# Second layer's gate and up projections as 20 units of seven block products, with the sums made by VectorE

## The chip, the cores and the metric

One Trainium2 chip, one of its cores. The metric is the device time of one launch in microseconds, lower is better. Engines are called as in the profile: PE (TensorE), DVE (VectorE), ACT (ScalarE), POOL (GpSimd), SP (SyncE, which only issues loads here).

## The reference, cut to what matters

Four transformer-like layers in fp32 over 512 tokens of width 1024. The change lies in the feed-forward part of the second one (`layer_c`):

```python
def swiglu(h, wg, wu, wd):
    return (jax.nn.silu(h @ wg) * (h @ wu)) @ wd
...
    h = modulate(x, norm_ffn, sh_f, sc_f)
    return x + g_f[:, None, :] * swiglu(h, wg, wu, wd)
```

`wg` and `wu` are 1024x2816, `wd` is 2816x1024. `modulate` is an RMS norm with a gain, a scale and a shift for each channel.

## The kernel before, in words

**Layout.** Activations lie transposed, channels on partitions: `x` is 8 blocks (k) of 128 channels by 512 tokens. Each weight comes as a panel of 128 output channels and 8 k-blocks, 128x1024 on chip (512 KB). A ring of four slots holds `raw`, `w_hi` and `w_lo`.

**Precision.** Each product is made of three matmuls in the fast fp32r format (L679 to L681): w_hi with h_hi, w_hi with h_lo, w_lo with h_hi. hi is the rounded value, lo the rest. ACT makes `w_hi` from `raw` (`split_hi`, L1226), POOL makes `w_lo = raw - w_hi` (`split_lo`, L603), and the activations' parts come from ACT (`h_hi`, `g_hi`) and DVE (`h_lo`, `g_lo`).

**What sets the order.** Every engine runs an order written out by hand, in step through counting semaphores. SP loads panel p+4 once `lo_ready` has reached p+1. ACT splits it once PE is done with the slot's old panel (`panel_done`). PE waits for `lo_ready` and for `bank_free` of the PSUM bank p % 4.

**The feed-forward part.** 22 tiles of 128 hidden channels go in parts of 8, 8 and 6. A part has first a gate and an up panel for each tile (`panels`, 48 matmuls of 512 columns for a pair), then 8 down panels over the part's tiles. For a tile ACT takes SiLU of the gate's bank (L1283), DVE multiplies it with the up bank (L1776), ACT rounds the product to `g_hi` (L1291), DVE takes the rest to `g_lo` (L1791). `add_x` (L1702) adds a down panel to `x`. At the start of the part DVE's `norm_h` makes the normalized `tn`, ACT `h_hi` (L1252), DVE `h_lo` (L1686), k by k, and PE goes through three panels at once (`by_k`), then the fourth. POOL only splits here. The loads of three constants of the third layer (`wsT`, `rows`, `bs`) are issued by ACT before the second layer's output projection; POOL's `affine_select` (L658) waits for them after the last down panel.

## Time and profile before

| | us |
|---|---|
| median of 3 runs (lowest, highest) | 2456.07 (2455.55, 2458.01) |
| profiled execution, span | 2452.9 |
| PE busy | 2386.9 (97%) |
| DVE, ACT, POOL busy | 1291.4, 951.4, 1097.8 |
| mean granted TensorE clock | 0.986 |

The profiled execution's time is its span, from the first to the last instruction; the runs' times are of whole launches. PE's busy time counts pipelined matmuls that overlap; how fast they follow each other is read from their starts.

### The profile page before, as it was taken

To read this page: it belongs to the slowest core of one execution; us is meant where nothing else is said; L and a number is where in the kernel's file an instruction comes from. 1 tells how busy PE (TensorE), PEld (TensorE's weight loads), DVE (VectorE), ACT (ScalarE), POOL (GpSimd) and SP (SyncE) were. 2 spreads that over 40 slices of the span, in tenths; PEclk is the share of its full clock that TensorE was granted. 3 is DMA by queue.
4 is the path that set the end of the run, shared out by engine and by line. 5 is a ranking of instruction groups with operands and counts; after the bars stand their busy time and mean duration, and the time that the engine had idled before them with its cause. 6 is when DMAs were issued, how large, how long until landed. Compare 5 with 4: busy or idle time off the path is not lost.

```text
span 2452.9 us, 34883 instructions
## 1 busy us (share of the span) xinstructions
PE 2386.9 (97%) x11957; PEld 1933.5 (79%) x11957; DVE 1291.4 (53%) x2318; ACT 951.4 (39%) x1554; POOL 1097.8 (45%) x529
## 2 busy tenths in 40 slices
PE   7999999999999999999999999999999999999998
PEld 6776778888876577888888678888888968888887
DVE  6777564443248753111147966454567474635455
ACT  3458332222335834222235454222246384422222
POOL 2336334444535543444455733444354464444433
PEclk9999999999999999999999999999999999999999
DMA  7531335554222022222222212322232201232222
GB/s 301 203 129 53 129 138 191 186 179 146 103 78 86 19 86 77 95 94 95 102 99 91 78 68 104 108 91 101 94 112 95 95 19 61 86 111 94 96 93 77
DMA packets 64196, 261.54 MB, mean 107 GB/s; under 512 B 7248, under 2 KB 7760, under 8 KB 57936
## 3 DMA queue, kind: packets, MB, share of 16 engines
q1 hardware_dynamic: 61056, 251.00, 28.8%
q10 hardware_dynamic: 3024, 8.98, 1.0%
q8 instruction: 74, 1.21, 0.2%
q14 instruction: 42, 0.34, 0.0%
HBM read 257.86 MB, written 2.10 MB: 106 GB/s over the span
## 4 chain that ended last, share of the span: by engine, by line
PE 88%; DVE 5%; issue 3%; POOL 1%; ACT 1%; DMA 1%; POOLq 1%; DVEq 0%; SPq 0%; ACTq 0%
PE bank L679 26%; PE bank L680 26%; PE bank L681 26%; PE bank L872 2%; PE bank L862 2%; PE bank L891 2%; POOL w_lo L603 1%; DMA first_mods<-in_first 1%; DVE acc L1639 1%; POOLq L667 1%; DVE bank L2268 1%; DVE bank L1908 1%; PE bank L804 1%; PE bank L700 1%; POOL prob L620 0%
## 5 line engine op out<-in xcount | busy, mean ns | idle before, releaser
L603 POOL TENSOR_TENSOR w_lo<-raw,w_hi 128x1024 fp32r<-128x1024 f32 x378 | 917.5, 2435 | 1219.0 <-ACT w_hi L1226 1217.3
L679 PE MATMUL bank<-h_hi,w_hi 128*128 128x512 f32 x1760 | 698.2, 397 | 13.8 <-DVE h_lo L1686 7.8
L680 PE MATMUL bank<-h_lo,w_hi 128*128 128x512 f32 x1760 | 690.4, 392 | 0.0
L681 PE MATMUL bank<-h_hi,w_lo 128*128 128x512 f32 x1760 | 690.3, 392 | 0.0
L1226 ACT ACTIVATE w_hi<-raw 128x1024 fp32r<-128x1024 f32 x378 | 392.5, 1051 | 424.3 <-PE bank L681 421.5
L679 PE MATMUL bank<-g_hi,w_hi 128*128 128x512 f32 x1072 | 418.5, 390 | 0.0
L681 PE MATMUL bank<-g_hi,w_lo 128*128 128x512 f32 x1072 | 417.2, 389 | 0.0
L680 PE MATMUL bank<-g_lo,w_hi 128*128 128x512 f32 x1072 | 417.1, 389 | 0.0
L679 PEld LDWEIGHTS bank<-h_hi,w_hi 128*128 128x128 f32 x1760 | 333.9, 190 | 94.9 <-DVE h_lo L1686 8.7
L681 PEld LDWEIGHTS bank<-h_hi,w_lo 128*128 128x128 f32 x1760 | 333.6, 190 | 71.5
L680 PEld LDWEIGHTS bank<-h_lo,w_hi 128*128 128x128 f32 x1760 | 333.7, 190 | 68.0 <-issue 0.5
L681 PEld LDWEIGHTS bank<-g_hi,w_lo 128*128 128x128 f32 x1072 | 201.2, 188 | 42.4
L679 PEld LDWEIGHTS bank<-g_hi,w_hi 128*128 128x128 f32 x1072 | 201.2, 188 | 41.5 <-issue 0.2
L680 PEld LDWEIGHTS bank<-g_lo,w_hi 128*128 128x128 f32 x1072 | 201.3, 188 | 41.3
L1776 DVE TENSOR_TENSOR prod<-silu,bank 128x512 f32<-128x512 f32 x44 | 30.2, 687 | 304.0 <-PE bank L681 303.8
L620 POOL TENSOR_TENSOR prob<-prob,stat 128x1024 f32<-128x1024 f32 (+1 forms) x96 | 120.0, 1253 | 90.7 <-DVE stat L1826 56.8
L1291 ACT ACTIVATE g_hi<-prod 128x512 f32 x66 | 41.7, 632 | 300.9 <-DVE prod L1776 197.3
L1702 DVE SCALAR_TENSOR_TENSOR x<-bank,plain,x 128x512 f32<-128x512 f32 x64 | 47.6, 748 | 156.8 <-PE bank L681 156.8
L1908 DVE SCALAR_TENSOR_TENSOR bank<-modraw,csil,bank 128x256 f32<-128x256 f32 x222 | 108.6, 489 | 16.9 <-issue 0.4
L1312 ACT ACTIVATE prob<-prob,stat 128x512 f32<-128x512 f32 (+1 forms) x192 | 106.7, 558 | 27.1 <-DVE stat L1816 26.6
L1702 DVE SCALAR_TENSOR_TENSOR x<-bank,modv,x 128x512 f32<-128x512 f32 x64 | 47.3, 748 | 120.7 <-PE bank L681 119.9
L1816 DVE CUSTOM_DVE_ANT_0 prob<-bank,mask 128x512 f32<-128x512 f32 (+1 forms) x192 | 90.2, 486 | 37.2 <-PE bank L862 33.7
(299 smaller groups left out, 2542.6 us busy)
## 6 DMA issues: line engine op xcount, KB each, us to landing
raw<-in_panels SPq DMA_DIRECT2D x378, 512.0 KB, 3.5
modraw<-in_pairs SPq DMA_DIRECT2D x40, 1024.0 KB, 5.6
first_mods<-in_first SPq DMA_DIRECT2D x4, 2048.0 KB, 22.2
x<-in_x SPq DMA_DIRECT2D x1, 2048.0 KB, 9.5
w<-in_w ACTq DMA_DIRECT2D x1, 2048.0 KB, 8.4
out<-yout ACTq DMA_DIRECT2D x8, 256.0 KB, 2.2
mask<-in_causal ACTq DMA_DIRECT2D x1, 1024.0 KB, 4.8
mask<-in_dilated ACTq DMA_DIRECT2D x1, 1024.0 KB, 7.5
```

Of the source, the lines that this page charges most:

```text
L603: pool.tensor_tensor(w_lo[:, slot, :], raw[:, slot, :], w_hi[:, slot, :].bitcast(F32), ALU.subtract)\
L620: pool.tensor_tensor(both, both, stat[:, 2, u:u + 2].rearrange("p (b o) -> p b o", o=1) .broadcast_to((P, 2, w)), ALU.mult).then_inc(weigh ...
L679: pe.matmul(out, w_h, m_h, start=start, stop=False)
L680: pe.matmul(out, w_h, m_l, start=False, stop=False)
L681: return pe.matmul(out, w_l, m_h, start=False, stop=stop)
L862: pe.matmul(score_bank(run, n, b)[:, 0:w], q_of(run, pairs_[n], b), k_of(run, pairs_[n], b), start=True, stop=True).then_inc(score_ready, 1)
L872: m = pe.transpose(bank[2 + b][:, P * j:P * j + P], prob[:, PROB_SLOT[n % PROB_STEPS], b, P * j:P * j + P], ident[:, :])
L1226: act.activation(w_hi[:, slot, :], raw[:, slot, :], ACT.Copy).then_inc(hi_ready, 1)
L1312: act.activation(row, row, ACT.Exp, bias=stat[:, 0, u % 64:u % 64 + 1], scale=-1.0, accum_out=stat[:, 1, u % 64:u % 64 + 1]).then_inc(exp_ ...
L1702: dve.scalar_tensor_tensor(out=x[:, n, :], in0=bank[p % RING][:, :], scalar=scale_by, in1=x[:, n, :], op0=MUL, op1=ADD).then_inc(bank_free, 1)
L1816: dve.tensor_tensor_reduce(row_of(n, b, w), score_bank(run, n, b)[:, 0:w], mask[:, i, 0:w], -SCALE, HIGHEST, ADD, ALU.min, stat[:, 0, u % ...
L1908: m = dve.scalar_tensor_tensor(out=part if k < KB - 1 else to, in0=w[:, :, k, :], scalar=csil[:, k:k + 1], in1=part, op0=MUL, op1=ADD)
```

## The change

The gate and up panels of a tile, stacked, are a matrix of 1024x256. It is cut in four: B11 and B21 are the gate panel's k-blocks 0 to 3 and 4 to 7, B12 and B22 the same of the up panel. The activations are cut by k in the same way, and the 512 tokens into early and late halves. Where four blocks times four blocks need eight block products, Strassen's algorithm (here with shared sums) needs seven, P1 to P7, each of 4 k-blocks, 3 matmuls a block and 256 columns. The first four panels (two tiles) stay as they were; the other 20 tiles are units (6, 8 and 6 in the three parts).

- DVE makes four differences of weight blocks for each unit, into `wdiff`, one unit ahead (`weight_sums`).
- ACT and POOL split seven 128x512 halves for a unit, P1, P2 and P3's from `raw`, the other four from `wdiff` (`half_high`, `half_low`).
- Once, after the norm, DVE makes four sums of the normalized activations (now kept whole in `tn8`) and their lo parts, ACT their hi parts (`activation_sums`, `sums_high`).
- PE goes P7, P2, P6, P1 of the next unit, P5, P4, P3. P1 goes to bank X and is copied by ACT to bank Y (seed); P2 completes X, the early gate. P6 is added to Y. ACT copies P7 to `seventh`; DVE adds it to Y into bank Z (waited for by `third_ready`); P4 completes Z, the late gate. P5 is added to Y; DVE adds `seventh` again, which gives `late_up`; P3 completes Y, the early up part.
- The three constant loads are issued by ACT behind the last unit.

```diff
+UNITS = (PARTS[0] - PLAIN_FIRST // 2,) + PARTS[1:]
+ORDER = ("P1", "P7", "P2", "P6", "P5", "P4", "P3")
...
+        WDIFF = {"P5": 0, "P7": 1, "P6": 2, "P4": 3}
...
+        def weight_half(part, name, u):
+            p = unit_panel(part, u)
+            if name in WDIFF:
+                return wdiff[u % 2][:, WDIFF[name], :]
+            of, at = {"P1": (0, 0), "P2": (0, 1), "P3": (1, 1)}[name]
+            return raw[:, (p + of) % RING, KH * P * at:KH * P * at + KH * P]
...
-            split_from(P_OUT1 + RING, P_AG - P_OUT1 - RING)
+            split_from(P_OUT1 + RING, P_FFN1 + PLAIN_FIRST - P_OUT1 - RING)
+            def half_low(part, name, u):
+                source = weight_half(part, name, u)
+                hi, lo = half_of(w_hi, name), half_of(w_lo, name)
+                if name == "P3":
+                    pool.wait_ge(hi_ready, unit_panel(part, u) + 2)
+                    pool.tensor_tensor(lo, source, hi.bitcast(F32), ALU.subtract).then_inc(lo_ready, 2)
+                else:
+                    pool.wait_ge(half_hi, made(part, name, u) + 1)
+                    pool.tensor_tensor(lo, source, hi.bitcast(F32), ALU.subtract).then_inc(half_lo, 1)
+            for part, n in enumerate(UNITS):
+                down = unit_panel(part, n)
+                for name in ORDER:
+                    half_low(part, name, 0)
+                for u in range(n):
+                    last = u == n - 1
+                    if u == 0:
+                        half_low(part, "P1", 1)
+                    if not last:
+                        half_low(part, "P7", u + 1)
+                        half_low(part, "P2", u + 1)
+                        half_low(part, "P6", u + 1)
+                        if u + 2 < n:
+                            half_low(part, "P1", u + 2)
+                        half_low(part, "P5", u + 1)
+                        half_low(part, "P4", u + 1)
+                        half_low(part, "P3", u + 1)
+                split_from(down, KB)
...
+            def product(part, name, u, out, fresh=False):
+                if name == "P3":
+                    pe.wait_ge(lo_ready, unit_panel(part, u) + 2)
+                else:
+                    pe.wait_ge(half_lo, made(part, name, u) + 1)
+                (m_hi, m_lo), wh, wl = moving_of(name), half_of(w_hi, name), half_of(w_lo, name)
+                for k in range(KH):
+                    ks = slice(P * k, P * k + P)
+                    pe.matmul(out, wh[:, ks], m_hi[:, k, :], start=(fresh and k == 0), stop=False, skip_group_check=True)
+                    pe.matmul(out, wh[:, ks], m_lo[:, k, :], start=False, stop=False, skip_group_check=True)
+                    m = pe.matmul(out, wl[:, ks], m_hi[:, k, :], start=False, stop=(k == KH - 1), skip_group_check=True)
+                if name == "P3":
+                    m.then_inc(panel_done, 2)
+                else:
+                    m.then_inc(half_used, 1)
...
+            def units(part):
...
+                if part == 0:
+                    for out in (Y_BANK[0], Z_BANK):
+                        pe.matmul(bank[out][:, :], h_hi[:, 0, 0:P], h_hi[:, 0, :], start=True, stop=True)
+                first_product(part, 0)
+                for u in range(n):
+                    x_out, y_out = unit_out(X_BANK[u % 2]), unit_out(Y_BANK[u % 2])
+                    pe.wait_ge(sum_lo, 1)
+                    if before + u:
+                        pe.wait_ge(seventh_copied, before + u)
+                    product(part, "P7", u, unit_out(SEVENTH_BANK), True)
+                    pe.wait_ge(seeded, before + u + 1)
+                    product(part, "P2", u, x_out)
+                    pe.wait_ge(sum_lo, 3)
+                    product(part, "P6", u, y_out)
+                    if u + 1 < n:
+                        first_product(part, u + 1)
+                    pe.wait_ge(third_ready, before + u + 1)
+                    product(part, "P5", u, y_out)
+                    product(part, "P4", u, unit_out(Z_BANK))
+                    pe.wait_ge(sum_lo, 4)
+                    pe.wait_ge(late_up_ready, before + u + 1)
+                    product(part, "P3", u, y_out)
...
+            def half_high(part, name, u):
...
+                if name in WDIFF:
+                    order = ("P7", "P5", "P6", "P4").index(name)
+                    act.wait_ge(wdiff_ready, 4 * (units_before(part) + u) + order + 1)
+                else:
+                    p = unit_panel(part, u) + (name == "P3")
+                    act.wait_ge(raw_landed[p % RING], 16 * (p // RING + 1))
+                m = act.activation(half_of(w_hi, name), weight_half(part, name, u), ACT.Copy)
+                if name == "P3":
+                    m.then_inc(hi_ready, 2)
+                else:
+                    m.then_inc(half_hi, 1)
...
+                seed(0)
+                for u in range(n):
+                    f, last = unit_tile(part, u), u == n - 1
+                    if u == 0:
+                        half_high(part, "P1", 1)
+                    act.wait_ge(half_used, used(part, "P7", u) + 1)
+                    if before + u:
+                        act.wait_ge(late_up_ready, before + u)
+                    act.activation(seventh[:, :], unit_out(SEVENTH_BANK), ACT.Copy).then_inc(seventh_copied, 1)
+                    if not last:
+                        half_high(part, "P7", u + 1)
...
+                    if f % PARTS[0]:
+                        tile_high(f - 1)
+                    act.wait_ge(half_used, used(part, "P2", u) + 1)
+                    act.activation(silu[:, f % 2, 0:HALF], unit_out(X_BANK[u % 2]), ACT.Silu).then_inc(early_silu, 1)
+                    if not last:
+                        half_high(part, "P2", u + 1)
+                        half_high(part, "P6", u + 1)
+                        seed(u + 1)
+                        if u + 2 < n:
+                            half_high(part, "P1", u + 2)
+                        half_high(part, "P5", u + 1)
...
+                    act.wait_ge(half_used, used(part, "P4", u) + 1)
+                    act.activation(silu[:, f % 2, HALF:T], unit_out(Z_BANK), ACT.Silu).then_inc(silu_ready, 1)
+                    if not last:
+                        half_high(part, "P4", u + 1)
+                        half_high(part, "P3", u + 1)
...
-            act.dma_start(wsT[:, :, :], A["wsT"]).then_inc(layer2_landed, 16)
-            act.dma_start(rows[:, :, :], A["rows"]).then_inc(layer2_landed, 16)
-            act.dma_start(bs[:, :, :], A["bs"]).then_inc(layer2_landed, 16)
             project(P_OUT1, 3)
             take_root(3)
             h_high(3)
-            ffn(1, P_FFN1, 3)
+            sums_high()
+            ffn_by_units(P_FFN1)
...
+            def weight_sums(part, u):
+                p, before = unit_panel(part, u), units_before(part) + u
+                for q in (p, p + 1):
+                    dve.wait_ge(raw_landed[q % RING], 16 * (q // RING + 1))
+                if u >= 2:
+                    dve.wait_ge(half_lo, made(part, "P4", u - 2) + 1)
+                to = wdiff[u % 2]
+                b11, b21 = (raw[:, p % RING, KH * P * w:KH * P * w + KH * P] for w in range(2))
+                b12, b22 = (raw[:, (p + 1) % RING, KH * P * w:KH * P * w + KH * P] for w in range(2))
+                dve.tensor_tensor(to[:, WDIFF["P7"], :], b22, b12, SUB).then_inc(wdiff_ready, 1)
+                dve.tensor_tensor(to[:, WDIFF["P5"], :], b12, b11, SUB).then_inc(wdiff_ready, 1)
+                dve.drain()
+                dve.tensor_tensor(to[:, WDIFF["P6"], :], b22, to[:, WDIFF["P5"], :], SUB).then_inc(wdiff_ready, 1)
+                dve.drain()
+                dve.tensor_tensor(to[:, WDIFF["P4"], :], b21, to[:, WDIFF["P6"], :], SUB).then_inc(wdiff_ready, 1)
+            def sum_low(n, of):
+                dve.wait_ge(sum_hi, n)
+                hi = sum4[:, 0, :, :] if of == 4 else sums_hi[:, of - 1, :, :]
+                to = sum4[:, 1, :, :] if of == 4 else sums_lo[:, of - 1, :, :]
+                dve.tensor_tensor(to, sum_a[of][:, :, :], hi.bitcast(F32), SUB).then_inc(sum_lo, 1)
+            def activation_sums():
+                late = slice(HALF, T)
+                at = MOD + 3 * KB
+                dve.tensor_tensor(shift12[:, :], modv[:, at:at + KH], modv[:, at + KH:at + KB], ADD)
+                dve.tensor_tensor(sum_a[3][:, :, :], tn8[:, 0:KH, 0:HALF], tn8[:, 0:KH, late], SUB).then_inc(sum_made, 1)
+                dve.drain()
+                for k in range(KH):
+                    m = dve.scalar_tensor_tensor(out=sum_a[1][:, k, :], in0=tn8[:, k, late], scalar=shift12[:, k:k + 1],
+                                                 in1=tn8[:, KH + k, late], op0=ADD, op1=ADD)
+                m.then_inc(sum_made, 1)
+                sum_low(1, 3)
+                dve.drain()
+                for k in range(KH):
+                    m = dve.scalar_tensor_tensor(out=sum_a[2][:, k, :], in0=sum_a[1][:, k, :], scalar=shift(3, k),
+                                                 in1=tn8[:, k, 0:HALF], op0=SUB, op1=SUB)
...
+                sum_low(3, 2)
+                dve.drain()
+                sum_low(4, 4)
...
+            def units(part):
+                n, before = UNITS[part], units_before(part)
+                def finish(u):
+                    f = unit_tile(part, u)
+                    dve.wait_ge(panel_done, unit_panel(part, u) + 2)
+                    dve.wait_ge(early_silu, before + u + 1)
+                    dve.tensor_tensor(prod[:, f % 2, 0:HALF], silu[:, f % 2, 0:HALF], unit_out(Y_BANK[u % 2]), MUL)\
+                        .then_inc(bank_free, 2)
+                    dve.wait_ge(silu_ready, FC + f + 1)
+                    dve.tensor_tensor(prod[:, f % 2, HALF:T], silu[:, f % 2, HALF:T], late_up[:, :], MUL).then_inc(prod_ready, 1)
+                for u in range(n):
+                    f = unit_tile(part, u)
+                    if u:
+                        finish(u - 1)
+                    if u + 1 < n:
+                        weight_sums(part, u + 1)
+                    if u or part == 0:
+                        tile_low(f - 1)
+                    dve.wait_ge(half_used, used(part, "P6", u) + 1)
+                    dve.wait_ge(seventh_copied, before + u + 1)
+                    if before + u:
+                        dve.wait_ge(silu_ready, FC + f)
+                    dve.tensor_tensor(unit_out(Z_BANK), unit_out(Y_BANK[u % 2]), seventh[:, :], ADD).then_inc(third_ready, 1)
+                    dve.wait_ge(half_used, used(part, "P5", u) + 1)
+                    dve.tensor_tensor(late_up[:, :], unit_out(Y_BANK[u % 2]), seventh[:, :], ADD).then_inc(late_up_ready, 1)
+                    dve.drain()
+                finish(n - 1)
+                dve.drain()
+                tile_low(unit_tile(part, n - 1))
+                dve.drain()
```

**On DVE**, one steady unit. Before, the loop's second tile and its end (`prod` is SiLU times the up bank):

```order
L1774 REGISTER_ALU
L1775 REGISTER_ALU [waits silu_ready]
L1776 TENSOR_TENSOR prod<-silu,bank 128x512 [waits panel_done]
L1791 ISA [waits f_hi_ready]
L1791 TENSOR_TENSOR g_lo<-prod,g_hi 128x512
L1770 REGISTER_ALU
L1770 COMPARE_AND_BRANCH
```

Now:

```order
L2185 TENSOR_TENSOR prod<-silu,bank 128x256 [waits early_silu,panel_done]
L2188 TENSOR_TENSOR prod<-silu,late_up 128x256 [waits silu_ready]
L2121 TENSOR_TENSOR wdiff_152<-raw 128x512 [waits half_lo,raw_landed1,raw_landed0]
L2122 TENSOR_TENSOR wdiff_152<-raw 128x512
L2124 TENSOR_TENSOR wdiff_152<-raw,wdiff_152 128x512
L2126 TENSOR_TENSOR wdiff_152<-raw,wdiff_152 128x512
L2166 TENSOR_TENSOR g_lo<-prod,g_hi 128x512 [waits f_hi_ready]
L2202 TENSOR_TENSOR bank<-bank,seventh 128x256 [waits silu_ready,seventh_copied,half_used]
L2204 TENSOR_TENSOR late_up<-bank,seventh 128x256 [waits half_used]
```

Between one tile's product and its g_lo now stand the four differences for the next unit, and the addition into Z comes behind g_lo.

**On ACT**, from the second layer's norm into the first units. Before:

```order
L1252 ACTIVATE h_hi<-tn,modv 128x512 [waits t_ready] x8
L1278 UNCONDITIONAL_BRANCH
L1278 ISA
L1283 ACT_TABLE_LOAD
L1283 ACTIVATE silu<-bank 128x512 [waits panel_done]
L1222 ISA
L1226 ACTIVATE w_hi<-raw 128x1024 [waits panel_done,raw_landed2]
```

Now:

```order
L1437 ACTIVATE h_hi<-tn_144,modv 128x512 [waits t_ready] x8
L1487 ACTIVATE sums_hi<-sum_147 128x1024 [waits sum_made]
L1487 ACTIVATE sums_hi<-sum_145 128x1024 [waits sum_made]
L1487 ACTIVATE sums_hi<-sum_146 128x1024 [waits sum_made]
L1487 ACTIVATE sum_150<-sum_147 128x1024 [waits sum_made]
L1498 ACT_TABLE_LOAD
L1498 ACTIVATE silu<-bank 128x512 [waits panel_done]
L1476 ACTIVATE w_hi<-raw 128x512 [waits raw_landed2,panel_done]
L1476 ACTIVATE w_hi<-wdiff_151 128x512 [waits wdiff_ready,panel_done]
L1476 ACTIVATE w_hi<-raw 128x512 [waits raw_landed2,panel_done]
```

The four hi parts of the sums and the table load for SiLU now stand ahead of the first SiLU and of the first halves' hi parts.

**On POOL**, the second layer's splits. Before, the loop over panels and what follows it:

```order
L603 TENSOR_TENSOR w_lo<-raw,w_hi 128x1024 [waits hi_ready]
L602 REGISTER_ALU
L603 TENSOR_TENSOR w_lo<-raw,w_hi 128x1024 [waits hi_ready]
L602 REGISTER_ALU
L603 TENSOR_TENSOR w_lo<-raw,w_hi 128x1024 [waits hi_ready]
L602 REGISTER_ALU
L603 TENSOR_TENSOR w_lo<-raw,w_hi 128x1024 [waits hi_ready]
L608 REGISTER_ALU
L608 COMPARE_AND_BRANCH
L658 ISA
L658 AFFINE_SELECT wsT<-wsT 128x1024 [waits layer2_landed]
```

Now, from the last plain panels to P1 and P7 of unit 1:

```order
L693 TENSOR_TENSOR w_lo<-raw,w_hi 128x1024 [waits hi_ready]
L698 REGISTER_ALU
L698 COMPARE_AND_BRANCH
L756 TENSOR_TENSOR w_lo<-raw,w_hi 128x512 [waits half_hi]
L756 TENSOR_TENSOR w_lo<-wdiff_151,w_hi 128x512 [waits half_hi]
L756 TENSOR_TENSOR w_lo<-raw,w_hi 128x512 [waits half_hi]
L756 TENSOR_TENSOR w_lo<-wdiff_151,w_hi 128x512 [waits half_hi] x3
L753 TENSOR_TENSOR w_lo<-raw,w_hi 128x512 [waits hi_ready]
L756 TENSOR_TENSOR w_lo<-raw,w_hi 128x512 [waits half_hi]
L756 TENSOR_TENSOR w_lo<-wdiff_152,w_hi 128x512 [waits half_hi]
```

Where one subtraction for a panel stood, a unit has seven of half the size, and all seven of unit 0 stand ahead of the first of unit 1 (the row after L753).

## Rows read from the trace of the kernel before

**Rows 1.** The page, part 1: busy us (share of the span) xinstructions

```profile
PE 2386.9 (97%) x11957; PEld 1933.5 (79%) x11957; DVE 1291.4 (53%) x2318; ACT 951.4 (39%) x1554; POOL 1097.8 (45%) x529
```

**Rows 2.** The page, part 4: the chain that ended last, by line

```profile
PE bank L679 26%; PE bank L680 26%; PE bank L681 26%; PE bank L872 2%; PE bank L862 2%; PE bank L891 2%; POOL w_lo L603 1%; DMA first_mods<-in_first 1%; DVE acc L1639 1%; POOLq L667 1%; DVE bank L2268 1%; DVE bank L1908 1%; PE bank L804 1%; PE bank L700 1%; POOL prob L620 0%
```

**Rows 3.** Busy time by engine in a stretch of the second layer's feed-forward part

```profile
core 0: us, PE busy (x) PEld busy (x) DVE busy (x) ACT busy (x) POOL busy (x), PEclk, DMA share, GB/s
1000.00:1290.00 290.00, 290.00 (x1281) 240.15 (x1280) 56.36 (x72) 83.70 (x104) 129.38 (x56) 1.00 0.28 98
```

**Rows 4.** Timeline of PE, 512 columns: start, us; 36 matmuls apart

```profile
1179.67 0.39 PE L680 MATMUL bank<-g_lo,w_hi 128*128 128x512 f32 x1
...
1187.83 0.39 PE L680 MATMUL bank<-g_lo,w_hi 128*128 128x512 f32 x1
```

**Rows 5.** Timeline of PE, 256 columns (an earlier stage); 26 matmuls apart

```profile
723.83 0.28 PE L679 MATMUL bank<-w_hi,h_hi 128*128 128x256 f32 x1
...
726.95 0.28 PE L681 MATMUL bank<-w_hi,h_lo 128*128 128x256 f32 x1
```

**Rows 6.** Groups of instructions by shape, whole run: busy us, mean ns, idle before

```profile
L603 POOL TENSOR_TENSOR w_lo<-raw,w_hi 128x1024 fp32r<-128x1024 f32 x378 | 917.5, 2435 | 1219.0 <-ACT w_hi L1226 1217.3 <-issue 1.4
L634 POOL TENSOR_TENSOR h_lo<-ya,h_hi 128x512 fp32r<-128x512 f32 x4 | 5.1, 1274 | 0.0
L1776 DVE TENSOR_TENSOR prod<-silu,bank 128x512 f32<-128x512 f32 x44 | 30.2, 687 | 304.0 <-PE bank L681 303.8 <-issue 0.3
L1851 DVE TENSOR_TENSOR h_lo<-bank,h_hi 128x256 fp32r<-128x256 f32 x24 | 9.9, 411 | 2.2 <-ACT h_hi L1338 2.2
L1908 DVE SCALAR_TENSOR_TENSOR bank<-modraw,csil,bank 128x256 f32<-128x256 f32 x222 | 108.6, 489 | 16.9 <-issue 0.4
L1226 ACT ACTIVATE w_hi<-raw 128x1024 fp32r<-128x1024 f32 x378 | 392.5, 1051 | 424.3 <-PE bank L681 421.5 <-DMA raw<-in_panels 2.4
L1291 ACT ACTIVATE g_hi<-prod 128x512 f32 x66 | 41.7, 632 | 300.9 <-DVE prod L1776 197.3 <-DVE prod L1788 103.6
L1338 ACT ACTIVATE h_hi<-bank 128x256 fp32r<-128x256 f32 x24 | 8.9, 371 | 2.6 <-PE bank L891 2.6
```

**Rows 7.** Timelines of DVE and POOL where they meet: start, us

```profile
1272.46 2.87 DVE L1639 TENSOR_TENSOR acc<-acc,sq 128x512 f32<-128x512 f32 x1
1272.40 2.39 POOL L603 TENSOR_TENSOR w_lo<-raw,w_hi 128x1024 fp32r<-128x1024 f32 x1 [1.37 <-ACT w_hi L1226]
1282.09 1.40 DVE L1639 TENSOR_TENSOR acc<-acc,sq 128x512 f32<-128x512 f32 x1
1282.92 2.83 POOL L603 TENSOR_TENSOR w_lo<-raw,w_hi 128x1024 fp32r<-128x1024 f32 x1
951.84 0.69 DVE L1776 TENSOR_TENSOR prod<-silu,bank 128x512 f32<-128x512 f32 x1 [2.22 <-PE bank L681]
946.66 10.38 POOL L603 TENSOR_TENSOR w_lo<-raw,w_hi 128x1024 fp32r<-128x1024 f32 x4 [23.45 <-ACT w_hi L1226]
```

**Rows 8.** Timelines of DVE and ACT at the start of the part

```profile
936.53 1.59 DVE L1686 SCALAR_TENSOR_TENSOR h_lo<-tn,modv,h_hi 128x512 fp32r<-128x512 f32 x2
937.22 1.28 ACT L1283 ACT_TABLE_LOAD   x1
945.04 0.60 ACT L1283 ACTIVATE silu<-bank 128x512 f32<-128x512 f32 x1 [6.54 <-PE bank L681]
```

**Rows 9.** Gaps of PE, each with the stretch behind it (columns of rows 3)

```profile
337.23 0.61 PE L700 MATMUL bank<-ones,modsum 128*128 128x1 f32 x4 [1.97 <-DVE modsum L1908]
338.73:342.15 3.42, 3.42 (x10) 2.65 (x9) 0.69 (x1) 2.37 (x3) 2.25 (x1) 0.50 0.91 353
1411.72 1.12 PE L1140 MATMUL bank<-cout,ones 128*128 128x512 f32 x2 [2.25 <-DVE cout L2268]
1413.90:1417.30 3.40, 2.19 (x8) 1.37 (x9) 3.19 (x5) 0.63 (x1) 0.00 (x0) 1.00 0.00 0
```

More of the change, by code:

```diff
@@ L837, in ffn @@
                         begun = 4
-                    panels(p + begun, 2 * size - begun, *up, mods=p < MOD_UNTIL)
+                    if layer == 1:
+                        units(n)
+                    else:
+                        panels(p + begun, 2 * size - begun, *up, mods=p < MOD_UNTIL)
                     p += 2 * size
@@ L1301, in ffn @@
                     else:
[L1302 removed]
+                        project_folded(p, 8)
                     p += KB
```

183 lines of the change are left out of this document (176 added, 7 removed).

## The prediction

> **What bounds the kernel now.** I read the page's first part first: TensorE (PE) is busy 97% of the span [rows 1]. Then the chain that ended last: nearly four fifths of it are the three matmul lines of the hi/lo product [rows 2]. Then the stretch that the change touches, the second layer's feed-forward part, about 927 to 1300 us: from 1000 to 1290 PE is busy all of the time at the full granted clock, while VectorE (DVE) works 56 us of 290, ScalarE (ACT) 84 and GpSimd (POOL) 129 [rows 3]. No other engine is waited for there, so one microsecond of matmul taken out is one microsecond gained, as long as the others stay out of the way. The argument below is that they don't.
>
> **What PE saves.** A gate and up pair costs 2 x 8 x 3 = 48 matmuls of 512 columns. They start (1187.83 - 1179.67)/36 = 0.2267 us apart [rows 4], so a pair is 10.88 us. A unit has seven products of 4 x 3 = 12 matmuls with 256 columns, 84 in all. Such matmuls stand elsewhere in the trace: (726.95 - 723.83)/26 = 0.1200 us apart [rows 5], with a weight load before each, as here. A unit is then 10.08 us. A product is 1.44 us. Twenty units save 20 x 0.80 = 16.0 us; two extra 512-column matmuls ahead of the first unit cost 0.45.
> Halving the columns does not halve the spacing. The Trainium skill (TensorE: Matmul & The Clock Gate, "Back-to-back issue gap") gives N/2.4 + 2.5 ns, so 216 and 109 ns, which would save 20 x (10.36 - 9.17) = 24 us. The rows have some 11 ns more for each matmul, and a unit has 36 matmuls more than a pair; the rows decide, and by the page the sum below would be 8 us lower.
>
> **What the other engines get.** Per unit POOL gets seven subtractions of 128x512 in place of two of 128x1024. One such took 1.27 us against 2.44 [rows 6], so 8.9 us in place of 4.9. DVE gets four subtractions of weights from SBUF (0.69 each, by the 128x512 products of rows 6), two PSUM additions and two products of 256 columns (0.41 each), and keeps the 0.69 of g_lo: some 5.1 us. ACT gets seven 128x512 copies (0.63 each), four short PSUM passes (about 0.4) and g_hi: 6.6 us. Each engine alone fits into 10.08 us. Together DVE and POOL don't.
>
> **The wait between DVE and POOL.** A DVE addition with both inputs in SBUF, issued at 1272.46 just after a POOL subtraction had started, ended at 1275.33, 0.54 us after POOL's end at 1274.79; alone it takes 0.69. In the other direction, POOL's subtraction of 1282.92 ended at 1285.75, 2.26 us after the DVE addition before it (1283.49), in place of 2.40 from its own start [rows 7]. So the later one waits for the earlier one's end and then needs 0.54 (DVE) or its own time less 0.14 (POOL; 1.27 becomes 1.13). A DVE product with one input in PSUM took 0.69 beside POOL's row of four [rows 7]: those are not held.
> The Trainium skill says the same (SBUF — State Buffer, "Who interferes with whom": a DVE instruction with two SBUF inputs contends with a GpSimd instruction that reads SBUF, and the second fully blocks). By this rule, as by the rows, the change puts six such DVE instructions and seven such POOL ones into one unit: it speaks against the change.
>
> Now one steady unit, in time from the end of the previous unit's P3, which is when P7 starts. PE needs P7, P2, P6 and the next unit's P1, 5.76 us, before it asks for third_ready. DVE must do, in this order: early product 0.2 to 0.6 (0.2 is the tail of the last matmul); late product, held by POOL's P4 half until 1.1, ends 1.4; first weight subtraction, held by POOL's P3 half until 2.5, ends 3.1; second 3.8; third 4.5. POOL's P7 half (its hi part is ready near 3.9, since ACT needs the first subtraction for it) then takes its turn until 5.65; fourth subtraction 6.2; POOL's P2 half until 7.35; g_lo 7.9; the addition into Z 8.3. P5 can start at 8.45. PE has stood since 5.76: **2.7 us**. P5, P4, P3 follow, 4.32, so a unit is 12.8 us. Without POOL the same DVE row ends near 4.9 and PE never waits.
> The wait stands in every unit but the first of a part: there no product of a previous unit goes ahead (in the first part that unit is part of the start, below). In the last unit of a part there are no weight subtractions, but no next P1 either, so PE asks at 4.32 and g_lo comes after ACT's 1.05 us panel split: 2.3. That is 14 x 2.7 + 3 x 2.3 = **44.7 us**.
>
> **The start.** After the last h_lo (938.12) [rows 8] DVE makes the first unit's weight differences (4 x 0.69 with drains, 2.9), then the activation sums: up to the last of them three instructions over 1024 elements (no row of its own; 0.41 at 256 and 0.69 at 512 columns give 1.25) and three groups of four 128x256 steps (0.49 each, 1.9 a group), 12.4 in all, so 950.5. ACT then has the last sum's hi part (1.05), a table load (1.28; before, it ran at 937.22 where nobody waited), SiLU (0.60) and P1's hi half (0.63), and POOL 1.27: 955.5. PE ends the four plain panels 24 x 0.2267 after by_k's end at 945.04 [rows 8], at 950.5, and the two extra matmuls at 950.9. It waits **4.6 us**. Next, POOL has all seven halves of unit 0 ahead of P1 of unit 1: 7 more at 1.23 and some five DVE turns of 0.54 make 966.8, and PE, having done P1, P7, P2 and P6 as their halves come, wants it near 962 to 963: **4 us**.
>
> **The clock.** Granted clock falls to half (0.50, the 1.2 GHz level) after an idle PE: after the 1.97 us gap that ends at 337.23 it was 0.50 from 338.73 for 3.42 us; after the 2.25 us gap that ended at 1411.72 it stayed at 1.00 [rows 9]. The gaps here are 2.3 to 4.6 us long, so I take it for half of the 19 gaps, at half of 3.42 = 1.7 each: **+16**. Bounds: none 0, all 32.
>
> **Nothing, and what covers it.** The panels' loads are as many; SP now releases them in twos when P3's low half is done, 10 us before the first reader, against a landing of a few microseconds (DMA share 0.28 [rows 3]). The three layer-2 constant loads move behind the last unit, eight down panels ahead of POOL's wait for them; if that cover went, they would cost POOL about one landing. The down panels are unchanged; their first-panel waits for the last tile are covered by size-1 tiles, except in the last part, about 1 us.
>
> **Sum.** -16.0 + 0.5 + 44.7 + 4.6 + 4 + 16 + 1 = +54.8, of which I take 53, since a slow clock after a gap also gives POOL time. Span 2452.9 + 53 = 2506. The median of the runs, 2456.07, stands 3.1 above the profiled span, so **2509 us**.
>
> **Rivals.**
> A, only the shared turn counts. If DVE's turns fell where POOL waits for ACT anyway, the unit would be bound by the sum of turns, 5 x 0.54 + 0.27 + 7 x 1.13 = 10.9 us, as long as a pair before: with the start (9) and little clock, 2456 + 12 = 2468; between that and the forecast every mixture is possible. For it: turns may interleave better than I laid them out. Against: DVE's order is fixed, with third_ready last.
> B, every gap lowers the clock, and the halved PE makes the next unit's DVE work late too: +16 more, 2525.
> C, the other side: DVE is held at most once in a unit, since POOL's halves come when DVE waits for PE. Then third_ready comes before 5.76 + a little: -16 + 0.5 + 8.6 = 2449, faster. It decides where the held time per unit is under 0.9 us (5.76 - 4.9); rows 7 have single holds of 1.1 and more for a POOL half, and POOL is busy 8.9 of 10 us, so DVE's six instructions can hardly miss it.
> D, the POOL halves are the bound by themselves (if a 128x512 one costs more than 1.44 us when held back): then 7 x 1.68 (1.13 + 0.54) = 11.8 a unit, 2456 + 18 + 9 + some clock, 2490.
>
> **Numbers.** Forecast (2490 to 2522) 0.60; A and mixtures up to 2490 0.15; D 0.08, inside the lower end; B 0.08; C 0.06; nearly no change 0.03. The range, 2478 to 2528, takes in the forecast with clock losses from 0 to 32, D and most of B. A difference of 0.2%, 5 us, is what a measurement of this kernel can tell: faster 0.06, same 0.04, slower 0.90.
>
> **What would show it.** Right: in the stretch of the units PE idle before P5's first matmul, released by DVE's addition into bank 7, 2 to 3 us, in 17 units; DVE's weight subtractions with means over 1.1 us in place of 0.69; unit period near 12.8; one gap of 4 to 5 us near 951 released by POOL; new stretches of clock 0.50. Wrong: DVE two-input instructions at 0.7 us beside POOL, unit period under 11, or PE waiting for POOL's halves (rival D) rather than for DVE.

## The result, and the profile after

The changed kernel takes 2509.06 us (median of 4 runs, 2507.12 to 2510.97), the kernel before 2455.99 in the same comparison (2455.55 to 2458.01): ratio 1.0212, 95% interval 1.0199 to 1.0224. That is 53.1 us slower. The profiled executions, spans 2505.4 and 2452.9, stand 52.5 apart.

The page of the changed kernel, part 1 (it answers to [rows 1]):

```profile
PE 2394.4 (96%) x12679; PEld 1973.8 (79%) x12679; DVE 1439.5 (57%) x2476; ACT 1007.9 (40%) x1715; POOL 1210.0 (48%) x629
```

PE's busy time hardly grew; it now stands idle or runs slowly for some 50 us more. DVE is busy 148 us more and POOL 112; part of that is time in which they are held, as shown below. The same stretch as in [rows 3], busy time by engine, then one slow stretch within it:

```profile
1000.00:1290.00 290.00, 258.44 (x1688) 240.59 (x1687) 144.96 (x158) 109.67 (x203) 200.58 (x126) 0.95 0.27 88
```

```profile
1112.39:1115.81 3.42, 3.21 (x15) 3.21 (x16) 0.40 (x2) 0.24 (x1) 2.17 (x2) 0.50 0.00 0
```

PE was busy 290 of 290 us at clock 1.00 before; now 258 of 290 at a mean of 0.95. DVE went from 56 to 145 us and POOL from 129 to 201: neither is full. So what holds PE is an order of waiting, and the view of PE's waits in the feed-forward part, 925 to 1355 us, names it (waited for; us in total, times, longest):

```profile
PE bank L960 <- DVE bank L2202: 38.0, 17, 2.6
PE bank L960 <- POOL w_lo L756: 7.4, 2, 4.8
...
PE bank L799 <- DVE g_lo L2166: 0.8, 1, 0.8
```

L2202 is DVE's addition into bank Z, `third_ready`. PE waits for it exactly 17 times, in no first unit of a part. (The line left out was there before the change too.) PE's timeline at the first matmul of P5 in three units that follow one another:

```profile
1100.00 0.39 PE L960 MATMUL bank<-sums_hi,w_hi 128*128 128x256 f32 x1 [2.57 <-DVE bank L2202]
...
1112.60 0.58 PE L960 MATMUL bank<-sums_hi,w_hi 128*128 128x256 f32 x1 [2.27 <-DVE bank L2202]
...
1126.58 0.38 PE L960 MATMUL bank<-sums_hi,w_hi 128*128 128x256 f32 x1 [2.26 <-DVE bank L2202]
```

A unit is 12.60 us here at full clock, and 13.98 where, as behind 1112.60, the clock is at 0.50 (its 1.2 GHz level) right after the gap. Until 932 us the clock is at 0.50 before the change too. Behind that there are twelve slow stretches in the part, one of 6.8 us at 962 and eleven of 3.4; before there was none. Each of the eleven begins between 0.4 us before and 1.6 us after the end of one of the 17 gaps; the other six gaps, 1.9 to 2.6 us long like these, are followed by none, and nothing read here tells the two sorts apart.

The start of P7 in the unit between the first two of those gaps, then DVE in that unit and POOL beside it (the timelines of the three engines; they answer to [rows 7]):

```profile
1104.42 0.28 PE L960 MATMUL bank<-sums_hi,w_hi 128*128 128x256 f32 x1
```

```profile
1104.67 0.42 DVE L2185 TENSOR_TENSOR prod<-silu,bank 128x256 f32<-128x256 f32 x1 [2.51 <-PE bank L962]
1105.01 0.72 DVE L2188 TENSOR_TENSOR prod<-silu,late_up 128x256 f32<-128x256 f32 x1
1105.65 1.78 DVE L2121 TENSOR_TENSOR wdiff<-raw 128x512 f32<-128x512 f32 x1
1107.36 0.68 DVE L2122 TENSOR_TENSOR wdiff<-raw 128x512 f32<-128x512 f32 x1
1108.13 0.69 DVE L2124 TENSOR_TENSOR wdiff<-raw,wdiff 128x512 f32<-128x512 f32 x1
1108.92 1.61 DVE L2126 TENSOR_TENSOR wdiff<-raw,wdiff 128x512 f32<-128x512 f32 x1
1110.45 1.75 DVE L2166 TENSOR_TENSOR g_lo<-prod,g_hi 128x512 fp32r<-128x512 f32 x1
1112.13 0.42 DVE L2202 TENSOR_TENSOR bank<-bank,seventh 128x256 f32<-128x256 f32 x1
```

```profile
1104.16 1.29 POOL L756 TENSOR_TENSOR w_lo<-wdiff,w_hi 128x512 fp32r<-128x512 f32 x1 [0.42 <-ACT w_hi L1476]
1105.44 1.44 POOL L753 TENSOR_TENSOR w_lo<-raw,w_hi 128x512 fp32r<-128x512 f32 x1
1108.24 1.74 POOL L756 TENSOR_TENSOR w_lo<-wdiff,w_hi 128x512 fp32r<-128x512 f32 x1 [1.35 <-ACT w_hi L1476]
1109.95 1.71 POOL L756 TENSOR_TENSOR w_lo<-raw,w_hi 128x512 fp32r<-128x512 f32 x1
```

From the early product on DVE has no gap over 0.1 us. Three of its instructions with 512 columns are held: L2121 ends at 1107.43, 0.55 after POOL's end at 1106.88; L2126 at 1110.53, 0.55 after POOL's 1109.98; L2166 at 1112.20, 0.54 after POOL's 1111.66. So is the late product, L2188, of 256 columns: it took 0.72 in place of 0.42 and ended 0.28 after POOL's 1105.45. L2122 and L2124 fell where POOL waited for ACT, or began just ahead of its next one, and took their own 0.69; POOL's, held in turn, took 1.71 to 1.74 in place of 1.27. The groups by shape, whole part (busy us, mean ns, idle before), show the same over 20 units:

```profile
L2166 DVE TENSOR_TENSOR g_lo<-prod,g_hi 128x512 fp32r<-128x512 f32 x22 | 42.1, 1912 | 11.1 <-ACT g_hi L1493 11.1
L2121 DVE TENSOR_TENSOR wdiff<-raw 128x512 f32<-128x512 f32 x20 | 29.9, 1496 | 0.4 <-issue 0.4
L2126 DVE TENSOR_TENSOR wdiff<-raw,wdiff 128x512 f32<-128x512 f32 x20 | 29.4, 1472 | 1.8
L2122 DVE TENSOR_TENSOR wdiff<-raw 128x512 f32<-128x512 f32 x20 | 19.1, 957 | 0.0
L2124 DVE TENSOR_TENSOR wdiff<-raw,wdiff 128x512 f32<-128x512 f32 x20 | 18.0, 902 | 2.2 <-issue 0.4
L2188 DVE TENSOR_TENSOR prod<-silu,late_up 128x256 f32<-128x256 f32 x20 | 14.2, 709 | 0.0
```

The five instructions of 512 columns with both operands in SBUF should take 0.69 each [rows 6]; the addition from PSUM takes its 0.42 (L2202 in the timeline). The start, which answers to [rows 8]: the last sum's hi part on ACT, with the table load, SiLU and P1's hi half behind it, then PE's two waits for POOL:

```profile
948.80 1.06 ACT L1487 ACTIVATE sum<-sum 128x1024 fp32r<-128x1024 f32 x1 [1.84 <-DVE sum L2155]
```

```profile
953.70 0.38 PE L960 MATMUL bank<-h_hi,w_hi 128*128 128x256 f32 x1 [2.56 <-POOL w_lo L756]
...
964.71 0.55 PE L960 MATMUL bank<-h_hi,w_hi 128*128 128x256 f32 x1 [4.84 <-POOL w_lo L756]
```

### The profile page after: what moved, and what is told of

Its sections match the earlier page's. It is cut to its first block, busy times and chain, and to the rows that moved or that the text cites. A ratio compares the mean times of both kernels' runs of the same rounds, so it can differ in the third digit from the quotient of the medians.

```text
span 2505.4 us, 36734 instructions
## 1 busy us (share of the span) xinstructions
PE 2394.4 (96%) x12679; PEld 1973.8 (79%) x12679; DVE 1439.5 (57%) x2476; ACT 1007.9 (40%) x1715; POOL 1210.0 (48%) x629
## 4 chain that ended last, share of the span: by engine, by line
PE 81%; DVE 9%; issue 4%; POOL 2%; ACT 1%; DVEq 1%; DMA 1%; POOLq 1%; SPq 0%; ACTq 0%
PE bank L799 22%; PE bank L801 22%; PE bank L800 22%; PE bank L1057 2%; PE bank L1047 2%; PE bank L1076 2%; PE bank L960 2%; PE bank L961 2%; PE bank L962 2%; DVE g_lo L2166 1%; DVE wdiff L2121 1%; POOL w_lo L693 1%; DMA first_mods<-in_first 1%; DVE acc L1938 1%; POOLq L787 1%
## 5 line engine op out<-in xcount | busy, mean ns | idle before, releaser
L693 POOL TENSOR_TENSOR w_lo<-raw,w_hi 128x1024 fp32r<-128x1024 f32 x338 | 823.2, 2444 | 1060.2 <-ACT w_hi L1411 1058.9
L799 PE MATMUL bank<-h_hi,w_hi 128*128 128x512 f32 x1440 | 573.8, 398 | 13.8 <-DVE h_lo L1988 7.8
L800 PE MATMUL bank<-h_lo,w_hi 128*128 128x512 f32 x1440 | 565.9, 393 | 0.0
L801 PE MATMUL bank<-h_hi,w_lo 128*128 128x512 f32 x1440 | 565.5, 393 | 0.0
L1411 ACT ACTIVATE w_hi<-raw 128x1024 fp32r<-128x1024 f32 x338 | 350.5, 1051 | 393.5 <-PE bank L801 384.7
L799 PEld LDWEIGHTS bank<-h_hi,w_hi 128*128 128x128 f32 x1440 | 273.5, 190 | 82.2 <-issue 8.7
L801 PEld LDWEIGHTS bank<-h_hi,w_lo 128*128 128x128 f32 x1440 | 273.5, 190 | 58.9
L800 PEld LDWEIGHTS bank<-h_lo,w_hi 128*128 128x128 f32 x1440 | 273.6, 190 | 55.8 <-issue 0.5
L799 PEld LDWEIGHTS bank<-g_hi,w_hi 128*128 128x128 f32 x1072 | 201.3, 188 | 42.8 <-DVE g_lo L2166 1.2
L756 POOL TENSOR_TENSOR w_lo<-wdiff,w_hi 128x512 fp32r<-128x512 f32 x80 | 118.5, 1484 | 54.8 <-ACT w_hi L1476 54.8
L960 PE MATMUL bank<-sums_hi,w_hi 128*128 128x256 f32 x240 | 74.5, 310 | 38.0 <-DVE bank L2202 38.0
```

The costliest lines, as they stand in the source:

```text
L693: pool.tensor_tensor(w_lo[:, slot, :], raw[:, slot, :], w_hi[:, slot, :].bitcast(F32), ALU.subtract)\
L756: pool.tensor_tensor(lo, source, hi.bitcast(F32), ALU.subtract).then_inc(half_lo, 1)
L799: pe.matmul(out, w_h, m_h, start=start, stop=False)
L800: pe.matmul(out, w_h, m_l, start=False, stop=False)
L801: return pe.matmul(out, w_l, m_h, start=False, stop=stop)
L960: pe.matmul(out, wh[:, ks], m_hi[:, k, :], start=(fresh and k == 0), stop=False, skip_group_check=True)
```

## The experiments

The theory: DVE's instructions with both operands in SBUF and POOL's halves take turns; with `third_ready` behind six of them PE waits in every unit, and each wait can lower its clock besides. Eight kernels test that, in two comparisons with the kernel before (2456.88 us in the first, 2456.42 in the second).

**1. No weight differences.**

```diff
-            if name in WDIFF:
-                return wdiff[u % 2][:, WDIFF[name], :]
-            of, at = {"P1": (0, 0), "P2": (0, 1), "P3": (1, 1)}[name]
+            of, at = {"P1": (0, 0), "P2": (0, 1), "P3": (1, 1), "P4": (0, 1), "P5": (1, 0), "P6": (1, 1), "P7": (1, 0)}[name]
...
-                        weight_sums(part, u + 1)
...
```

> Leaves out the four weight differences of each unit on VectorE; the halves P4 to P7 are split from the raw blocks instead, so the output is not the reference's. All seven GpSimd halves, the activation sums and the order stay. Theory (VectorE and GpSimd take turns, and third_ready comes last): the differences are four of VectorE's six held instructions; without them third_ready comes near 4 us into the unit and PE no longer waits in the steady units (38.0 us of PE's waits in the units fall to under 3, of the 12 stretches of clock 0.50 between 960 and 1310 at most two remain). What stays is the wait of some 5 to 7 us at the start and the saving of 16: 2450 to 2457 us. Rival 1 (GpSimd's seven halves are a bound by themselves): PE waits for w_lo in the units, 2480 or more. Rival 2 (VectorE's chain behind PE, the additions and ACT's passes, is too long even with no differences): over 1.5 us of wait in each unit remains, 2480 or more.

Measured: 2456.39 us, ratio 1.0003 (0.9993 to 1.0012). PE's waits in the units, the second of them in the first unit:

```profile
PE bank L958 <- DVE bank L2194: 5.1, 8, 1.1
PE bank L958 <- POOL w_lo L754: 3.5, 1, 3.5
```

Both rivals fall: POOL still makes seven halves a unit and behind the first unit nobody waits for it, and the chain through ACT and the additions is short enough. The waits for DVE are 5.1 us where under 3 was expected: g_lo (1.40 us on average) is still held. Two slow stretches are left of the twelve, as expected.

**2. GpSimd's halves a quarter as long.**

```diff
-                    pool.tensor_tensor(lo, source, hi.bitcast(F32), ALU.subtract).then_inc(half_lo, 1)
+                    pool.tensor_tensor(lo[:, 0:P], source[:, 0:P], hi[:, 0:P].bitcast(F32), ALU.subtract).then_inc(half_lo, 1)
...
```

> GpSimd's seven subtractions of a unit work on 128 of their 512 columns; the rest of w_lo keeps old values, so the output is not the reference's. VectorE's instructions are all there. Theory (the turn with GpSimd): a difference is held for a quarter of the time, VectorE's four differences go back from 0.9 to 1.5 us each to 0.7 to 0.9, third_ready comes before PE asks for it; waits of PE in the units under 4 us in all, 2448 to 2456 us. Rival (VectorE has simply too much work ahead of the addition, whatever GpSimd does): the addition comes no more than 0.5 us earlier in a unit, PE's waits stay over 25 us, 2490 or more.

Measured: 2452.96 us, ratio 0.9984 (0.9975 to 0.9994). PE's waits for the addition, and one of DVE's groups:

```profile
PE bank L960 <- DVE bank L2202: 5.7, 3, 1.9
```

```profile
L2121 DVE TENSOR_TENSOR wdiff<-raw 128x512 f32<-128x512 f32 x20 | 13.8, 688 | 0.4 <-issue 0.4
```

DVE does all its work here, and PE waits for its addition only in the last unit of each of the three parts: 5.7 us, and 2.4 for others at the start, where under 4 was expected. DVE has not too much to do; it is held. One difference (L2122, 0.94 us on average) stayed a little above the 0.9 expected.

**3. The addition earlier.**

```diff
                 dve.drain()
+                if between is not None:
+                    between()
                 dve.tensor_tensor(to[:, WDIFF["P6"], :], b22, to[:, WDIFF["P5"], :], SUB).then_inc(wdiff_ready, 1)
...
+                    def third():
...
+                        dve.tensor_tensor(unit_out(Z_BANK), unit_out(Y_BANK[u % 2]), seventh[:, :], ADD).then_inc(third_ready, 1)
                     if u + 1 < n:
-                        weight_sums(part, u + 1)
-                    if u or part == 0:
-                        tile_low(f - 1)
...
+                        weight_sums(part, u + 1, third)
...
                     dve.tensor_tensor(late_up[:, :], unit_out(Y_BANK[u % 2]), seventh[:, :], ADD).then_inc(late_up_ready, 1)
+                    if u or part == 0:
+                        tile_low(f - 1)
```

> Nothing left out. On VectorE the addition into bank Z (third_ready) moves from behind the four differences and g_lo to between the second and the third difference; the addition for late_up comes behind the fourth, g_lo last. The same work and the same turns. Theory (it is the place of the addition behind the held instructions that costs): the wait of 2.2 us in 17 units goes or falls under 0.7 us, and with it most of the slow stretches (12 now): 2455 to 2466 us. Rival 1 (the sum of turns bounds the unit, 10.9 us or more): the wait moves to another instruction, PE waits for w_lo or late_up by 0.8 us or more a unit, 2470 to 2490. Rival 2 (the cost is mostly in the clock and the start, not in the wait): under 15 us gained, 2494 or more.

Measured: 2460.82 us, ratio 1.0016 (1.0007 to 1.0026), +3.9 us in place of +53.1, with the same instructions. PE's waits, busy time in a stretch of units, and DVE around the addition:

```profile
PE bank L960 <- POOL w_lo L756: 7.4, 2, 4.9
PE bank L960 <- DVE bank L2201: 5.6, 10, 0.6
```

```profile
1100.00:1150.00 50.00, 47.62 (x383) 46.11 (x383) 44.60 (x42) 25.32 (x54) 50.00 (x33) 1.00 0.31 106
```

```profile
1119.52 1.78 DVE L2122 TENSOR_TENSOR wdiff<-raw 128x512 f32<-128x512 f32 x1
1121.49 0.43 DVE L2201 TENSOR_TENSOR bank<-bank,seventh 128x256 f32<-128x256 f32 x1 [0.19 <-PE bank L962]
1121.84 1.15 DVE L2126 TENSOR_TENSOR wdiff<-raw,wdiff 128x512 f32<-128x512 f32 x1
```

The view names PE as what the addition waited for, but P6, which it reads, had ended near 1119.93; DVE was in the held second difference until 1121.30. PE waits 0.6 us for the addition. Of the 17 distances between units within the parts, eight are 11.1 to 11.2 us; in the stretch shown, where they are, POOL is busy 50.00 of 50 us. That is close to the 10.9 that the prediction's rival A worked out as the sum of turns. So the turns by themselves cost some 1.1 us in such a unit, and their place ahead of `third_ready` the other 1.4. Over all 17 distances, from the first late_up addition of a part to its last, it is 177.2 us against 167.0 of PE's own work: the turns cost 10 us, and their place some 33 of the 42.8 worked out further down.

**4. The start in another order.**

```diff
                     act.activation(to, sum_a[of][:, :, :], ACT.Copy).then_inc(sum_hi, 1)
+                    if n == 1:
+                        half_high(0, "P1", 0)
+                        half_high(0, "P7", 0)
+                    if n == 2:
+                        half_high(0, "P2", 0)
+                        half_high(0, "P6", 0)
...
-                half_high(0, "P1", 0)
-                half_high(0, "P7", 0)
-                half_high(0, "P2", 0)
-                half_high(0, "P6", 0)
```

> Nothing left out. Only the start: ACT makes the hi parts of the halves P1 and P7 of the first unit after the second sum's hi part, P2 and P6 after the third's, ahead of the table load and SiLU, in place of behind them. Theory: the first wait of PE for w_lo (about 4.8 us of 7.4) falls by 2 to 4 us, but the activation sums by VectorE come no earlier and PE waits for them instead, so the time falls by 0 to 4 us: 2505 to 2509. Rival (the start's order is what the change lost by, through the clock too): 8 us or more gained, 2501 or less.

Measured: 2510.90 us (2509.64 to 2512.24), no gain, and 1.9 above the range expected. The wait has moved, not gone; PE now waits for ACT's copy of bank X into Y, which stands behind the last sum's hi part, the table load and the plain tiles' SiLU:

```profile
PE bank L960 <- ACT bank L1521: 6.3, 1, 6.3
```

The sums themselves come later too. The four steps of the last sum on DVE, in the changed kernel and here:

```profile
947.10 1.67 DVE L2155 SCALAR_TENSOR_TENSOR sum<-tn,modv,sum 128x256 f32<-128x256 f32 x4
...
949.77 3.75 DVE L2157 SCALAR_TENSOR_TENSOR sum<-tn,modv,sum 128x256 f32<-128x256 f32 x4
```

Here POOL makes two halves beside them (950.24 to 953.24), and the sum before it took 3.74 in place of 1.67 beside two others: the turn again, some 4 us of it, in a place where the changed kernel had none.

**5. The gap filled.** Before `pe.wait_ge(third_ready, ...)`:

```diff
+                    if u:
+                        for _ in range(18):
+                            pe.matmul(bank[S0][:, 0:HALF], h_hi[:, 0, 0:P], h_hi[:, 0, 0:HALF], start=True, stop=True)
                     pe.wait_ge(third_ready, before + u + 1)
```

> The result stays the same; added are 18 matmuls of 256 columns (18 x 0.12 = 2.16 us) on data at hand, into an idle PSUM bank, ahead of PE's wait for third_ready in the 17 units that wait. Nothing else of the changed kernel is touched, so VectorE's addition still comes when it did. Theory (the granted clock falls because PE stands, and this costs some 12 to 18 us beside the waits themselves): PE's waits for VectorE shrink to a few us, the stretches of 0.50 inside the units go, a unit stays at 12.6 to 12.9 us, and the time falls to 2492 to 2500 us. Rival (the clock falls in this part for another reason, or its cost lies inside the waits and is no extra): the time stays at 2507 to 2512.

Measured: 2495.09 us (2494.36 to 2495.79), ratio to before 1.0162 (1.0145 to 1.0179), so +38.7 in place of +53.1: 306 matmuls that nobody needs make the kernel 14.4 us faster. PE's waits for the addition fall to 0.9 us. Busy time in the same stretch as above, and the late_up additions of four units (their first and last start):

```profile
1000.00:1290.00 290.00, 287.77 (x2034) 270.33 (x2033) 150.13 (x164) 115.70 (x213) 209.76 (x131) 1.00 0.27 90
```

```profile
L2207 DVE TENSOR_TENSOR late_up<-bank,seventh x4: 425/425/425, 1101.5 to 1139.4; 128x256 f32<-128x256 f32 x4
```

The clock is 1.00 throughout this stretch, and a unit is (1139.4 - 1101.5)/3 = 12.63 us, as in the changed kernel's units at full clock. This separates the two costs: the gaps, and the clock behind them. The traces say the same as the medians: from the first late_up addition to the last it is 319.9 us here (972.2 to 1292.1) and 333.9 in the changed kernel (969.8 to 1303.7), 14.0 less.

**6. Operands in PSUM.** VectorE's order as in the change.

```diff
+                of12, of22 = (COPY_BANK[0][:, :], COPY_BANK[1][:, :]) if copied else (b12, b22)
...
-                dve.tensor_tensor(to[:, WDIFF["P7"], :], b22, b12, SUB).then_inc(wdiff_ready, 1)
...
+                dve.tensor_tensor(to[:, WDIFF["P7"], :], b22, of12, SUB).then_inc(wdiff_ready, 1)
...
-                    dve.tensor_tensor(prod[:, f % 2, HALF:T], silu[:, f % 2, HALF:T], late_up[:, :], MUL).then_inc(prod_ready, 1)
+                    dve.tensor_tensor(prod[:, f % 2, HALF:T], unit_out(Z_BANK), late_up[:, :], MUL).then_inc(prod_ready, 1)
```

> Nothing left out. VectorE's and GpSimd's work and VectorE's order stay those of the changed kernel, the addition into bank Z last. ACT copies the up panel's halves B12 and B22 of the unit after next into two idle PSUM banks (two more passes of 0.63 us a unit), and the first three differences take one operand from there; the late SiLU is left in its PSUM bank, so the late product has one operand there too. VectorE has then two instructions with both operands in SBUF (the fourth difference and g_lo) in place of six. First units of a part (in the first part, the first two) keep the old differences. Theory (the turn between instructions with two SBUF operands and GpSimd's): those differences and the late product go back to 0.7 and 0.42 us beside GpSimd, third_ready comes 2 us earlier, waits of PE for it fall from 38 us to under 15, 2460 to 2472 us. Rival (VectorE is slowed beside GpSimd wherever its operands are, or the chain from PE through ACT is what is long): waits over 30 us, the more so since ACT has 1.3 us more in each unit; 2500 to 2515.

Measured: 2474.61 us (2472.19 to 2476.20), ratio 1.0082 (1.0065 to 1.0099); 2.6 above the range expected, but +18.2 in place of +53.1. PE's waits, DVE in one unit, and the one POOL half beside its first two differences:

```profile
PE bank L969 <- DVE bank L2230: 14.8, 17, 1.9
```

```profile
1119.51 0.68 DVE L2149 TENSOR_TENSOR wdiff<-raw,bank 128x512 f32<-128x512 f32 x1
1120.11 0.68 DVE L2150 TENSOR_TENSOR wdiff<-bank,raw 128x512 f32<-128x512 f32 x1
1120.88 0.69 DVE L2152 TENSOR_TENSOR wdiff<-bank,wdiff 128x512 f32<-128x512 f32 x1
1121.66 1.38 DVE L2154 TENSOR_TENSOR wdiff<-raw,wdiff 128x512 f32<-128x512 f32 x1
1122.97 1.78 DVE L2194 TENSOR_TENSOR g_lo<-prod,g_hi 128x512 fp32r<-128x512 f32 x1
```

```profile
1119.70 1.31 POOL L762 TENSOR_TENSOR w_lo<-raw,w_hi 128x512 fp32r<-128x512 f32 x1
```

The first two differences ran beside POOL's half in 0.68 each, and POOL's took 1.31, near its own 1.27. The two that still read SBUF twice are held. With VectorE's order and GpSimd's halves unchanged, it is the operands' place that decides. The Trainium skill (SBUF — State Buffer, "Who interferes with whom") says that a DVE instruction with at most one SBUF input does not contend with GpSimd; these rows agree. A unit is 10.99 us; the last units of a part keep waits of up to 1.9 us; the prediction put these down to g_lo, which there comes late from ACT, and no run tried it.

**7. Earlier addition and eight plain panels.** Experiment 3, and:

```diff
-PLAIN_FIRST = 4
+PLAIN_FIRST = 8
...
+                        if n == 0:
+                            panels(p + 4, PLAIN_FIRST - 4, *up)
                         units(n)
...
```

> Nothing left out. The earlier addition (as in e3_addition_earlier) and a start with eight plain panels in place of four (18 units), with the plain tiles' SiLU and products between the activation sums. Theory (the start's wait of 7.4 us comes from sums and seven halves that have too little cover): the two more pairs give 10.9 us x 2 of cover each for 0.8 us of saving lost, PE's waits for GpSimd at the start go and one of about 1.5 for the plain product comes; 6 to 9 us faster than e3_addition_earlier, so 2452 to 2455 us. Rival (the start's work just moves along with the first unit, whatever stands before it): a wait of 5 us or more ahead of the first unit's products again, 2459 or more.

Measured: 2450.98 us, ratio 0.9980 (0.9970 to 0.9989). PE's waits for POOL ahead of the first unit's products are gone, and 5.0 us in 9 waits for the addition stay. Less the difference of the two kernels before, that is 9.4 us better than experiment 3: a little more than the 6 to 9 expected, and the wait of 1.5 us for the plain product did not come.

**8. All three.** Experiments 6 and 7 together.

> Nothing left out. The PSUM operands, the earlier addition and the start with eight plain panels together. Theory: third_ready no longer waited for in steady units (only in the last unit of a part), unit 10.08 us, -14.4 us for 18 units, waits in the part under 8 us, clock 1.00 all through it: 2442 to 2449 us, faster than before by 0.3 to 0.6 per cent. Rival (ACT, with two more copies a unit, or GpSimd becomes what is waited for): 2453 or more.

Measured: 2445.40 us (5 runs, 2443.78 to 2446.24), ratio 0.9961 (0.9947 to 0.9975): 11.0 us faster than before, the fastest of all. Busy time in a stretch of units, PE's only waits for DVE's addition in the part, and the addition's groups of three units:

```profile
1090.00:1180.00 90.00, 89.48 (x588) 82.36 (x588) 37.04 (x55) 40.57 (x74) 65.71 (x43) 1.00 0.32 106
```

```profile
PE bank L969 <- DVE bank L2245: 1.6, 3, 0.5
```

```profile
L2253 DVE TENSOR_TENSOR late_up<-bank,seventh x3: 424/424/425, 1107.5 to 1127.7; 128x256 f32<-128x256 f32 x3
```

A unit is (1127.7 - 1107.5)/2 = 10.1 us: the seven products are paid at their own price, and of the 14.4 us that 18 units can save, 11.0 are there.

## Why the prediction was right

2509.0 was predicted, 2509.06 measured. That the total fits to the tenth is chance; the terms miss by up to 2 us, in both directions:

| term | predicted | measured |
|---|---|---|
| PE's saving, 20 x 0.80 | -16.0 | -16.0 (unit 10.08 in experiment 8) |
| two extra matmuls | +0.5 | not read apart |
| gap in 17 units | +44.7 | +42.8 |
| start | +8.6 | +7.4 |
| clock | +16 | +14.4 in the units, and up to 3.4 at the start |
| last part's down panels | +1 | +0.8 |
| sum | 54.8, of which 53 taken | 49.9 to 53.3, against 53.1 |

*PE's saving.* Right, from rows at two widths; experiment 8 shows 10.1 us a unit. By the formula of the Trainium skill (TensorE: Matmul & The Clock Gate, "Back-to-back issue gap") it would have been an estimated 9.17; the trace does not agree with it. The same section of the Trainium skill says that this formula under-counts at small N, because it has no room for the weight loads; each matmul here has one.

*The turn of DVE and POOL.* Right. The hand-made schedule had `third_ready` 8.3 us after the end of P3 and PE asking at 5.76; its pattern (late product and first difference held, second and third free, fourth and g_lo held) is the one in the timeline above. Counted from P7's start at 1104.42, DVE ended the late product, the four differences, g_lo and the addition at 1.3, 3.0, 3.6, 4.4, 6.1, 7.8 and 8.1, where 1.4, 3.1, 3.8, 4.5, 6.2, 7.9 and 8.3 were written. POOL's half of 1109.95 ended 1.13 us behind DVE's 1110.53, as reckoned. The 0.69 of a DVE instruction alone had been read from a product with one operand in PSUM; the differences of experiment 2, 0.688, bear it out for two operands in SBUF. The 42.8 comes from experiment 5, where the clock is 1.00: from the first late_up to the last, within the three parts, 61.3 + 86.9 + 61.6 = 209.8 us, of which PE's own work is 14 x 10.08 + 3 x 8.64 = 167.0. For a steady unit of a middle kind that is 2.55 against 2.7 predicted. The waits view says only 38.0 for the same 17 gaps, since it starts to count at the end of the last matmul, 0.28 after its start, where the next one could have started at 0.12, and leaves out the late start of the second matmul behind the gap (0.11): 0.27 us a gap, 4.6 in all.

*The start.* The sum was right, its halves not: 2.6 and 4.8 us where 4.6 and 4 were written. Two rows of DVE show why the first was shorter:

```profile
935.38 1.60 DVE L1988 SCALAR_TENSOR_TENSOR h_lo<-tn,modv,h_hi 128x512 fp32r<-128x512 f32 x2
...
941.30 1.68 DVE L2143 SCALAR_TENSOR_TENSOR sum<-tn,shift 128x256 f32<-128x256 f32 x4
```

The last h_lo ended at 936.98, 1.1 us earlier than in [rows 8], and the four steps of a sum over 256 columns take 1.68 us, 0.40 apart, where the prediction reckoned 1.9 from a row's duration of 0.49. So the last sum was there at 948.8 and not at 950.5. The second wait was taken too short by 0.8. In experiment 4 another order on ACT only moved the wait; experiment 7 shows that more cover takes it away.

*The clock.* "Half of the 19 gaps, 1.7 each" was the least certain step, a guess from two gaps of which one had been followed by 0.50 and one had not; that it came out is partly luck. Twelve slow stretches came, not nine or ten, but the eleven in the units cost 14.4 us, 1.3 each in place of 1.7. That part of a slow stretch lies in PE's wait, and that a slow PE gives DVE and POOL time, are the likely reasons; no run separates them.

*The rivals.* A (only the sum of turns) is what the earlier addition comes near, 11.2 us in its steady units. C (DVE held at most once) was refuted by the four holds in the unit shown. D (POOL's held halves the bound) was refuted for the changed kernel by the waits view: behind the start PE never waits for POOL there. In experiment 3, where POOL has no gap in a steady unit, A and D come to the same thing, and no run separates them. B would have needed 19 slow stretches.

## What to carry to other kernels

An algorithm that saves matmuls moves its additions to engines that share something: count for each unit the DVE instructions with both operands in SBUF and the GpSimd instructions beside them, and lay them out by hand in turns before believing that each engine "has room". Put the result that PE waits for ahead of those, or give one operand from PSUM; both, with more cover at the start, turned +53 us into -11. And where PE waits some 2 us in every unit, add the price of the clock: here a quarter of the loss.
